# Kernel with background work mixed into an expert stream: one slot at a time instead of four

## What is computed

```python
q = (xb @ p['peer_wq']).reshape(PEER_CHUNK, PEER_HEADS, 2, PEER_KEY_HALF)
s = jnp.einsum('thcd,ckd->thck', q, p['peer_subkeys']).astype(jnp.float32)
sv, si = lax.top_k(s, PEER_TOPK)
...
top_s, pos = lax.top_k(cand_s, PEER_TOPK)
eidx = jnp.take_along_axis(cand_i, pos, axis=-1).reshape(PEER_CHUNK, PEER_HEADS * PEER_TOPK)
gate = jax.nn.softmax(top_s, axis=-1).reshape(PEER_CHUNK, PEER_HEADS * PEER_TOPK).astype(xb.dtype)
u = jnp.take(p['peer_u'], eidx, axis=0)
v = jnp.take(p['peer_v'], eidx, axis=0)
act = jax.nn.gelu(jnp.einsum('ted,td->te', u, xb), approximate=False) * gate
return jnp.einsum('te,ted->td', act, v)
```

## Time and profile before

| | |
|---|---|
| median of 3 executions | 2873.32 us (2868.58 to 2879.14) |
| the profiled execution | 2877.59 us |
| its span in the trace | 2874.7 us |
| PE, DVE busy | 2136.9 us (74%), 1858.5 us (65%) |
| ACT, POOL busy | 1068.2 us (37%), 971.1 us (34%) |
| DMA | 976.16 MB, mean 340 GB/s |
| chain that ended last | PE 32%, DMA 27%, DVE 25%, issue 8%, ACT 5% |

### The profile page before, as it was taken

How to read it: one execution, slowest core, us unless ns; L and a number is a source line. 1 busy time by engine, 2 the same in 40 slices (tenths; PEclk the granted TensorE clock), 3 DMA queues, 4 the chain that set the end, 5 groups by cost and what they waited for, 6 DMA issues and landing times.

```text
span 2874.7 us, 25972 instructions
## 1 busy us (share of the span) xinstructions
PE 2136.9 (74%) x6768; PEld 1112.2 (39%) x6768; DVE 1858.5 (65%) x4482; ACT 1068.2 (37%) x2962; POOL 971.1 (34%) x916
## 2 busy tenths in 40 slices
PE   4987678769788878567668666767877787766665
PEld 2455444534444435334224332334453343433222
DVE  0135975964677659868876555552479585877775
ACT  2022453442355344334452243331235353433332
POOL 1011343323233233244353433420023343444553
PEclk9988889989888889788789889988888898888988
DMA  8467979979687689699999999995289889999997
GB/s 298 135 243 284 388 305 364 408 288 359 259 338 284 259 346 397 256 414 389 402 415 406 400 379 417 390 387 207 74 340 384 344 329 359 405 384 408 416 409 314
DMA packets 210711, 976.16 MB, mean 340 GB/s; under 512 B 17532, under 2 KB 70296, under 8 KB 112280
## 3 DMA queue, kind: packets, MB, share of 16 engines
q0 software_dynamic: 123648, 855.69, 74.2%
q1 hardware_dynamic: 86936, 118.99, 12.2%
HBM read 973.56 MB, written 1.05 MB: 339 GB/s over the span
## 4 chain that ended last, share of the span: by engine, by line
PE 32%; DMA 27%; DVE 25%; issue 8%; ACT 5%; POOL 2%; POOLq 0%; SPq 0%; DVEq 0%; ACTq 0%
DMA EXPERT<-in_peer_uv,FIX 26%; PE VS L919 11%; PE PA L788 10%; DVE EXPERT L1505 7%; DVE SCR L1146 3%; DVE ACC L1515 2%; POOL EXPERT L631 2%; PE PA L816 2%; PE PB L856 2%; PE VS L745 1%; PE PA L864 1%; PE PA L804 1%; ACT HT L1005 1%; DVE PICK L1488 1%; PE PA L719 1%
## 5 line engine op out<-in xcount | busy, mean ns | idle before, releaser
L919 PE MATMUL VS<-EXPERT,DIAG 128*128 128x512 f32 x2304 | 1157.4, 654 | 338.3 <-ACT DIAG L1101 324.4
L631 POOL DMA_INDIRECT EXPERT<-in_peer_uv,FIX x768 | 896.0, 1167 | 1075.7 <-PE VS L919 500.6
L1505 DVE CUSTOM_DVE_ANT_0 EXPERT<-EXPERT,H 128x1024 f32<-128x1024 f32 x768 | 924.9, 1223 | 412.0 <-DMA EXPERT<-in_peer_uv,FIX 404.5
L919 PEld LDWEIGHTS VS<-EXPERT,DIAG 128*128 128x128 f32 x2304 | 463.3, 210 | 981.2 <-issue 523.2
L1094 ACT ACTIVATE GEL<-DOT 128x1 f32<-128x1 f32 x768 | 155.3, 202 | 1027.2 <-DVE DOT L1505 1008.8
L788 PE MATMUL PA<-WT,HT 128*128 128x512 f32 (+2 forms) x768 | 338.9, 599 | 56.0 <-ACT QTD L1031 20.7
L1101 ACT ACTIVATE DIAG<-IDN,WEI 128x128 f32<-128x128 f32 x576 | 231.3, 402 | 116.7 <-PE VS L919 99.4
L1515 DVE SCALAR_TENSOR_TENSOR ACC<-EXPERT,WEI,ACC 128x1024 f32<-128x1024 f32 x192 | 245.8, 1280 | 2.7 <-ACT WEI L1096 2.1
L788 PEld LDWEIGHTS PA<-WT,HT 128*128 128x128 f32 x768 | 158.6, 210 | 222.6 <-issue 142.4
L1096 ACT ACTIVATE WEI<-GEL,GATE 128x1 f32<-128x1 f32 x768 | 226.3, 295 | 25.0
L623 POOL COPY FIX<-IDX 128x8 uint32 (+1 forms) x96 | 40.4, 421 | 501.2 <-PE VS L919 387.9
(11 more groups left out here) (141 smaller groups left out, 1740.8 us busy)
## 6 DMA issues: line engine op xcount, KB each, us to landing
EXPERT<-in_w_ada POOLq DMA_DIRECT2D x48, 1024.0 KB, 9.5
WT<-in_peer_wq SPq DMA_DIRECT2D x80, 512.0 KB
WT<-in_w_in SPq DMA_DIRECT2D x56, 512.0 KB
WT<-in_w_out SPq DMA_DIRECT2D x40, 512.0 KB
EXPERT<-in_peer_uv,FIX POOLq DMA_INDIRECT x768
WT<-in_w_in SPq DMA_DIRECT2D x16, 384.0 KB
WT<-in_w_in SPq DMA_DIRECT2D x20, 288.0 KB
WT<-in_mla_wk_up SPq DMA_DIRECT2D x5, 512.0 KB
```

The lines of the kernel that those rows point to most:

```text
L631: pool.indirect_dma_start(out=EXPERT[:, j, :], out_offset=None, in_=a["peer_uv"], in_offset=bass.IndirectOffsetOnAxis(ap=FIX[:, par, j:j + ...
L919: ins = nc.tensor.matmul(VSUM[n][:, :], DIAG[:, i, :], EXPERT[:, j, D + n * W:D + (n + 1) * W], start=first, stop=last_one)
L1505: nc.vector.tensor_tensor_reduce(out=EXPERT[:, j, 0:D], in0=EXPERT[:, j, 0:D], in1=H2[:, b % HB, :], scale=1.0, scalar=0.0, op0=ALU.mult, ...
```

## The change

The unit of the mix becomes one slot in place of one quad: `slots` stages replace `quads`, and the constants of the planner are multiplied by four (AHEAD 4 to 16). The background stages are cut smaller. `in` and `out` have four parts of one weight piece each, in place of two halves. `pick` is split into `pick` and `more`: on PE the first query half and the second, on ACT its copy, then the gate exponentials and the other copy, on DVE `top`, then `experts`. `also` is split in the same way into `also` and `then`. The costs of `out` go from 100 to 88 units a tile for its halves or parts together, of `also` from 80 to 85; the others keep their sums. `late` still moves the first unit of each run ahead, and that unit is now one slot. On PE, `release` comes behind the first addition of a run, not ahead of it. No arithmetic is added or left out.

```diff
-AHEAD = 4
+AHEAD = 16
...
-HALVES = ((0, KD // 2), (KD // 2, KD))
+PARTS = KD // KP
...
-        out += [("in", l, g, n, ts, half) for half in range(2)]
+        out += [("in", l, g, n, ts, part) for part in range(PARTS)]
...
-        out += [("gates", l, g, n, ts)] + [("out", l, g, n, ts, half) for half in range(2)]
+        out += [("gates", l, g, n, ts)] + [("out", l, g, n, ts, part) for part in range(PARTS)]
...
-        out.append(("pick", l, g, h, ts))
+        out += [("pick", l, g, h, ts), ("more", l, g, h, ts)]
         if h > 0 and len(ts) > 1:
-            out.append(("also", l, g, h, ts[1:]))
+            out += [("also", l, g, h, ts[1:]), ("then", l, g, h, ts[1:])]
...
-    return s[0] in ("in", "out") and s[-1] == 0
+    return s[0] in ("in", "out") and s[-1] < PARTS - 1
...
-    return s[0] == "pick" and s[3] > 0 and len(s[4]) > 1
+    return s[0] in ("pick", "more") and s[3] > 0 and len(s[4]) > 1
...
-COST = {"stat": (45, 0), "norm": (50, 0), "in": (0, 40), "turn": (0, 10), "root": (5, 5), "up": (0, 25), "attn": (35, 0),
-        "hnorm": (20, 0), "heads": (20, 0), "gates": (10, 0), "out": (0, 50), "back": (20, 0), "pick": (85, 0), "also": (80, 0),
+COST = {"stat": (45, 0), "norm": (50, 0), "in": (0, 20), "turn": (0, 10), "root": (5, 5), "up": (0, 25), "attn": (35, 0),
+        "hnorm": (20, 0), "heads": (20, 0), "gates": (10, 0), "out": (0, 22), "back": (20, 0), "pick": (45, 0), "more": (40, 0), "also": (45, 0), "then": (40, 0),
...
-    if stage[0] not in ("pick", "also") or stage[3] == 0:
+    if stage[0] not in ("more", "then") or stage[3] == 0:
         return []
     _, l, g, h, ts = stage
-    return [blocks_of(l, g)[ts[0]] * QUADS + 4 * (h - 1)]
+    return [blocks_of(l, g)[ts[0]] * SLOTS + TOPK * (h - 1)]
...
-        while at < to and picked(stream[at]) and not (stream[at][0] == "close" and (s[0] in ("in", "out") and s[-1] == 0
-                                                                                    or splits_pick(s))):
+        while at < to and picked(stream[at]) and not (stream[at][0] == "close" and (holds(s) or splits_pick(s))):
...
-            first, at, jumped = ("quads", b, q0, q0 + 1), len(out), 0
+            first, at, jumped = ("slots", b, q0, q0 + 1), len(out), 0
             while run > 0 and jumped < LEAD and put_off(out[at - 1], first):
                 at, run, jumped = at - 1, run - 1, jumped + cost(out[at - 1])
             if at == len(out):
                 out.append(s)
             else:
                 out.insert(at, first)
-                out += [("quads", b, q0 + 1, q1)] if q1 > q0 + 1 else []
+                out += [("slots", b, q0 + 1, q1)] if q1 > q0 + 1 else []
```

The functions on the engines follow:

```diff
-                if half == 1:
+                w = piece()
+                for t, bank in zip(ts, held["banks"]):
+                    for k in range(KP * part, KP * part + KP):
...
+                        if t == ts[0] and k % KP == 0:
+                            release()
...
+                    held["w"] = [head_piece() for k in range(0, KD, HP)]
+                    key_query(stage, 0)
+
+            def more(stage):
+                _, l, g, h, ts = stage
+                if h < PH:
+                    key_query(stage, 1)
                     owed.append((filled_b, rb.n, KD // HP))
...
+            def key_query(stage, c):
+
+                _, l, g, h, ts = stage
+                mine = slice(ts[0] * P, (ts[-1] + 1) * P)
...
-            def quads(stage):
-                _, b, q0, q1 = stage
-                release()
-                for kind, v0, v1 in parts_of(q0, q1):
+            def slots(stage):
+                _, b, i0, i1 = stage
+                for kind, v0, v1 in parts_of(i0, i1):
...
+                    elif v0 % 4 < BY_PE:
...
+                        apply((b * QUADS + v0 // 4) * BY_PE + v0 % 4, v0 % 4, slot_no(b, v0) % RING, first=(v0 == 0),
+                              last_one=(v0 == SLOTS - 1 - (4 - BY_PE)))
+                        release()
...
             def pick_(stage):
+                key_query(stage, 0)
+
+            def more(stage):
                 _, l, g, h, ts = stage
                 if h >= 1:
                     gate_exps(ts[0])
+                key_query(stage, 1)
+
...
                     return
                 top(ts[0])
-                experts(l, g, h - 1, ts[0])
+
+            def more(stage):
+                _, l, g, h, ts = stage
+                if h > 0:
+                    experts(l, g, h - 1, ts[0])
 
             def also(stage):
+                top(stage[4][0])
+
+            def then(stage):
                 _, l, g, h, ts = stage
-                top(ts[0])
                 experts(l, g, h - 1, ts[0])
```

More of the change, by code:

```diff
@@ L244, in spans @@
     for s in plan:
[L245 to L246 removed]
+        if s[0] == "slots" and out and out[-1][0] == "slots" and out[-1][1] == s[1] and out[-1][3] == s[2]:
+            out[-1] = ("slots", s[1], out[-1][2], s[3])
         else:
@@ L249, in spans, with stream_of @@
     return out
-def stream_of(b, first=0, last=QUADS):
-    return [("quads", b, q, q + 1) for q in range(first, last)] + ([("close", b)] if last == QUADS else [])
+def stream_of(b, first=0, last=SLOTS):
+    return [("slots", b, i, i + 1) for i in range(first, last)] + ([("close", b)] if last == SLOTS else [])
 def make_plan():
@@ L278, in make_plan @@
     first, picks = pick(1, LAT, (0,)), pick(1, LAT, (1,))
-    plan += first[:2]
-    rest = first[2:] + front(1, LAT, (1,), keys=False) + attention(1, LAT, 1) + outward(1, LAT, (1,)) + picks[:3]
-    plan += weave(plan, rest, stream_of(4, 0, QUADS - AHEAD))
-    plan += weave(plan, picks[3:], stream_of(4, QUADS - AHEAD) + [("last", 0)] + stream_of(5, 0, QUADS - 2 * AHEAD))
-    plan += stream_of(5, QUADS - 2 * AHEAD) + [("last", 1)]
+    plan += first[:4]
+    rest = first[4:] + front(1, LAT, (1,), keys=False) + attention(1, LAT, 1) + outward(1, LAT, (1,)) + picks[:6]
+    plan += weave(plan, rest, stream_of(4, 0, SLOTS - AHEAD))
+    plan += weave(plan, picks[6:], stream_of(4, SLOTS - AHEAD) + [("last", 0)] + stream_of(5, 0, SLOTS - 2 * AHEAD))
+    plan += stream_of(5, SLOTS - 2 * AHEAD) + [("last", 1)]
     at = {s: n for n, s in enumerate(plan)}
@@ L294, with put_off @@
 LEAD = 130
-def put_off(stage, quads):
-    return stage[0] in COST and not any(at <= quads[1] * QUADS + quads[3] - 1 + AHEAD for at in picks_of(stage))
+def put_off(stage, slots):
+    return stage[0] in COST and not any(at <= slots[1] * SLOTS + slots[3] - 1 + AHEAD for at in picks_of(stage))
 def late(plan):
@@ L324, in late @@
     for s in out:
-        if s[0] == "quads":
-            need = s[1] * QUADS + (s[3] - 1) // 4 * 4
-            assert any(at[p] < at[s] for p in out if need in picks_of(p)), "quads before their pick"
+        if s[0] == "slots":
+            need = s[1] * SLOTS + (s[3] - 1) // TOPK * TOPK
+            assert any(at[p] < at[s] for p in out if need in picks_of(p)), "slots before their pick"
     return out
@@ L774, in product @@
             def product(stage):
-                kind, l, g, name, ts, half = stage
+                kind, l, g, name, ts, part = stage
                 n = CHUNKS[name][1] if kind == "in" else W
-                if half == 0:
+                if part == 0:
                     if kind == "out":
@@ L943, in _ @@
             do = {"consts": consts, "ada": ada, "adat": adat, "norm": norm, "back": back, "in": product, "out": product,
-                  "up": up, "turn": turn, "attn": attn, "heads": heads, "pick": pick_, "quads": quads, "close": close}
+                  "up": up, "turn": turn, "attn": attn, "heads": heads, "pick": pick_, "more": more, "slots": slots,
+                  "close": close}
             for stage in PLAN:
@@ L1122, in _ @@
             do = {"consts": consts, "adae": adae, "stat": stat, "norm": norm, "root": root, "turn": turn, "attn": attn,
-                  "hnorm": hnorm, "heads": heads, "pick": pick_, "also": also, "quads": quads, "last": last_}
+                  "hnorm": hnorm, "heads": heads, "pick": pick_, "more": more, "then": then, "slots": slots,
+                  "last": last_}
             for stage in late(PLAN):
@@ L1241, in in_ @@
             def in_(stage):
-                _, l, g, what, ts, half = stage
-                if half == 0:
+                _, l, g, what, ts, part = stage
+                if part < PARTS - 1:
                     return
@@ L1400, in out_ @@
             def out_(stage):
-                _, l, g, n, ts, half = stage
-                if half == 0:
+                _, l, g, n, ts, part = stage
+                if part < PARTS - 1:
                     return
@@ L1571, in _ @@
                   "in": in_, "out": out_, "gates": gates, "up": up, "root": root, "turn": turn, "attn": attn,
-                  "hnorm": hnorm, "heads": heads, "pick": pick_, "also": also, "quads": quads, "close": close, "last": last_}
```

(2 more changed lines are left out.)

142 lines of the change are left out of this document (63 added, 79 removed).

## The result

The changed kernel takes 2963.47 us (median of 4 runs, 2960.96 to 2969.66) against 2874.77 us before (2868.58 to 2879.14): ratio 1.0313, 95% interval 1.0288 to 1.0339. I had forecast 2856 us and a range up to 2930. It is slower by 3.1%, outside the range, and on the other side.

A forecast was written before the change was run, and what follows sets the result against it. Gathers on DMA set the pace from 1210 to 1512 us; in six other stretches PE is busiest and waits behind DVE's batches. Terms 24 - 36 - 24 + 19 = -17 us, 2873.3 - 17 = 2856 us; range 2795 to 2930.

The forecast's parts named there:

- A: Rival, chance 0.26: PE waits for a diagonal behind every run of two, old waits outside attention stay; +39 us, 2912 us.
- Attention steps next to each other: First weave and layer 1 attention: a slot behind every step gives PE work during DVE's copy; 39 us of waits go.
- The second slot of a run: Four woven attentions: with one slot ahead, PE waits for the second slot's diagonal; +63 us, bounds 40 and 85.
- Key search: Key-search stages: same work stage for stage, small shifts mostly under full DMA; 0 us, bounds -15 and +20.
- Other stages: 610 to 1210 us: nine PE waits for gate rows, tiles and copies each 4 us shorter; -36 us, bounds 0 and -60.
- Ends of projections: 610 to 1069 us: slots not first in their run wait behind DVE's rotations or copies; +19 us, bounds 5 and 35.
- Close of block 1: Where block 1 closes: last slot and `close` stand together, regaining lost transfer time; -20 us, -4 at context picks' end.
- Table loads: ACT: 62 more loads at 1.28 us, 80 us of ACT, costed at nothing beyond those in the second slot's chain.
- rival D: Chance 0.04: every switch of ACT table costs its drain too, 40 us over the sum, 2896 us.
- Rival B: Chance 0.15: gathers always run, DMA rises from 0.8 to 0.9 in six stretches; half of 142 us gained, 2802 us.
- the sum: Whole kernel: all terms added, -17 us, 2856 us for the median; chance 0.40.

## Why the prediction was wrong

The rival that came true is A, the lost head start. I gave it 0.26 and a price of 2912 us, 51 us too low. Only its first half holds: PE waits for diagonals more than 63 us in the attentions, but the old waits outside did not keep their length, as A had it; they went, and waits for diagonals took their place. Step by step:

- *Attention steps next to each other, -39.* Right: the waits of the earlier trace rows at the value matmuls are gone from PE's list, those at the scores are down to 0.3 us in the latents. One reading was off: the 5.3 us in the earlier trace rows is a wait for ACT's exponential, not for a copy that DVE makes.
- *The second slot of a run, +63.* Right mechanism, undersized. PE's waits for diagonals in the attentions:

```profile
PE VS L924 <- ACT DIAG L1114: 25.9, 12, 5.4
...
PE VS L924 <- ACT DIAG L1114: 41.0, 27, 5.3
...
PE VS L924 <- ACT DIAG L1114: 36.1, 16, 4.7
```

  (362 to 447, 864 to 1050 and 2344 to 2470 us; total, times, longest) sum to 103 us, over the upper bound of 85 and over the 63 from which I had said that A decides. There are 55 waits, where I had counted 23 places, and 35 runs of two. I had let the first slot of every run pass as ready; with more waits than runs of two, it was not. The latent attentions are 4 us longer than 182, not 10 to 25; the layer 1 attention is 25 us longer than 101.
- *Key search, 0.* **This is the step that failed.** I called it stage for stage the same work, and had priced a run of two only in attention. But of the 42 runs of slots that stand behind a stage of the three searches for one tile, 36 have two slots or more. At 21 of them the second slot's dot stands on DVE behind a whole `top`, 5.07 us, and at 15 behind `experts`, some 3.3 us (in the head shown above, 585.27 to 588.61). PE's waits for diagonals in the three stretches after (259 to 362, 502 to 665, 2161 to 2298 us):

```profile
PE VS L924 <- ACT DIAG L1114: 34.3, 11, 5.7
...
PE VS L924 <- ACT DIAG L1114: 53.5, 15, 6.8
...
PE VS L924 <- ACT DIAG L1114: 45.7, 15, 7.4
```

  and before (264 to 351, 468 to 610, 2108 to 2221 us):

```profile
PE VS L919 <- ACT DIAG L1101: 5.7, 3, 4.5
...
PE VS L919 <- ACT DIAG L1101: 8.7, 6, 5.2
...
PE VS L919 <- ACT DIAG L1101: 20.2, 6, 8.1
```

  That is 134 us against 35. Not all of the 99 us are time: PE waited 34 us there for the copies of the queries before (10.9 + 14.3 + 8.7) and waits 0.4 us now. Over all producers its waits rise from 93 to 134 us, 41 more, and its busy time from 243 to 271 us, 28 more, which is the +61 to within the few slots by which the stretches differ. The run with two slots ahead over the search stages gives back 71 us, 57 of them in these three stretches (103 to 91, 163 to 138, 137 to 117 us). My bounds were -15 and +20. I had also taken most of the search as hidden under full DMA, and two of the three stretches did have it, 1.02 and 1.00. With two slots ahead they take 89 and 113 us, so they gain nothing from the finer order, but they can lose by it: DMA fell to 0.88 and 0.89 there with the change, and 40 of the 61 us are in these two.
- *Other stages, -36.* The waits went as I said: for gate rows PE waits 5.7 us between 665 and 864 us and 5.7 between 1148 and 1290, nothing between, 11.4 us against 34.7, and those for single tiles are nearly gone. No time came of it: this term failed too. In the projections of the latents 29.6 us of waits for diagonals took their place, in their output projection 19.5, where there were none before; with all producers PE waits 37 us in the projections, against 36 before. The finer order moved the wait from one release to another. With the head start back, the gain is there: two slots ahead over the stages other than search and attention is 40 us faster.
- *Ends of projections, +19.* These are the same 29.6 + 19.5 us: right mechanism, more than twice the size, since it happens not only at the ends.
- *Close of block 1, -24.* Half right. POOL's wait of 17.2 us is gone; that of 14.5 us is there unchanged, against my "no wait above 8 us". The emptiest 35 us around it, to set beside the earlier trace rows:

```profile
1258.00:1293.00 35.00, 22.97 (x73) 14.74 (x74) 25.86 (x68) 8.24 (x25) 9.01 (x9) 0.76 0.72 280
```

  DMA is idle 35 x 0.28 = 10 us of it, not 21, and the wait that stayed is this one of POOL, until PE has added a slot of the block:

```profile
1275.86 0.19 POOL L620 COPY FIX<-IDX 128x8 uint32 x1 [14.49 <-PE VS L924]
```

  The latents' key search around it is 16 us shorter.
- *Table loads, 0.* The load follows the operation before it at once here too (in the attention of layer 1 it starts at 2385.23, and the read-out ends at 2384.93 + 0.19 = 2385.12), so rival D, a drain at each switch, finds no support; this trace, like the one before, shows only the load's own 1.28 us. The Trainium skill, ScalarE: Activation LUTs, section on what ACT_TABLE_LOAD costs, adds a drain of about the same length; neither trace has it, and the idle time before the 115 loads at GELU (third group of the page above) sums to 6.0 us. But the loads are in the chain of a wanted diagonal: 0.37 us each with one slot ahead. For the 62 added ones that would be 23 us, an estimate from the mean over all.
- *Rival B, the mixing fills DMA, 2802 us.* The mechanism exists: with two slots ahead DMA goes from 0.78 to 0.93 in the first attention, from 0.85 to 0.96 in that of layer 1, and the kernel takes 2761 us. In the changed kernel the lost head start outweighs it. My argument against it, that PE has no more than 15 to 20% to give, was no bound: in the latent attentions PE's busy time itself fell from 155 us to 134.

I chose the sum (0.40) over A since nine old waits "have no other explanation". They had none, but removing a wait gains nothing when the same engine waits for another producer right behind it.

## What to carry to other kernels

When the unit of a background stream is made smaller, look for what else is counted in that unit: here the head start of the producing engines was one unit, and fell from four slots to one. Size it in time, not in units: as an estimate from this case, the consumer should have work for about as long as the longest foreground stage on the producer's queue plus the chain behind it. Here that is 5.1 + 2.2 = 7.3 us, from the timeline above; one slot and the queries give PE at most 1.9 + 2.0 us, two slots and the queries 5.8 us. Two did not end the waits for diagonals, but four gained no more time. Price the second unit behind every kind of stage, the longest first. A stretch that DMA fills may have nothing to gain from a new order, and still lose by it. Where waits shift from one producer to another, take the sum over all producers, and the busy time with it: waits for diagonals grew by 304 us here, all idle time of PE by 40.

## What was not expected of the hardware

A wait of PE costs more than its length. In PE's timeline of the changed kernel in the key search, slots of four matmuls:

```profile
561.35 1.88 PE L924 MATMUL VS<-EXPERT,DIAG 128*128 128x512 f32 x4
568.29 3.78 PE L924 MATMUL VS<-EXPERT,DIAG 128*128 128x512 f32 x4 [5.05 <-ACT DIAG L1114]
...
589.09 1.88 PE L924 MATMUL VS<-EXPERT,DIAG 128*128 128x512 f32 x4
591.89 1.98 PE L924 MATMUL VS<-EXPERT,DIAG 128*128 128x512 f32 x4 [0.91 <-ACT DIAG L1114]
```

The slot behind a wait of 5.05 us takes 3.78 us, twice 1.88; behind 0.91 us of waiting there is no such loss. The clock (last column but two) says why: it is 1.00, the level of 2.4 GHz, in the slot before the wait, and 0.50, that of 1.2 GHz, in the slot behind it.

```profile
561.40:563.20 1.80, 1.80 (x6) 0.53 (x4) 1.80 (x15) 0.27 (x1) 1.38 (x2) 1.00 0.99 368
...
568.40:572.00 3.60, 3.60 (x5) 1.53 (x6) 3.25 (x14) 2.58 (x6) 0.00 (x0) 0.50 0.99 414
```

Over the run PE is busy 2190.0 us with the change and 2125.4 with two slots ahead, for the same 6768 matmuls, and the granted clock in the search of layer 1 is 0.77 and 0.87. So up to 65 of the 203 us, and up to 53 of the 93 against the kernel before, may be the clock that falls behind the pauses, and not the pauses themselves. In the latent attentions, where two slots ahead over attention gave a clock of 1.00, the same matmuls took 125 us of PE instead of 142. I had counted waits at their length only; no run here changes the clock without the waits, so how much of the end it moves stays open.
